# Ten weight slots in place of eight, GpSimd's transfers on SyncE's queue, and one weight split ahead of the memory scaling

## The reference

```python
xt = rms_norm(x, g_ffn)
logits = xt @ w_router + b_router            # 256 x 32
top_v, top_e = lax.top_k(logits, 4)
wts = softmax(top_v)
# for each expert e with its tokens:
hdn = xblk @ w_mlp1[e] + b_mlp1[e]           # 1024 -> 2048
x_glu = minimum(hdn[:, ::2], 7);  x_lin = clip(hdn[:, 1::2], -7, 7)
act = x_glu * sigmoid(1.702 * x_glu) * (x_lin + 1)
y += wts * (act @ w_mlp2[e] + b_mlp2[e])     # 1024 -> 1024
```

## Time and profile before

| what | value |
|---|---|
| median of 3 runs | 1199.2 us |
| the profiled execution | 1199.93 us |
| its span, first to last instruction | 1198.0 us (1.9 us lie around it) |
| TensorE matmul busy | 1151.2 us, 96% |
| VectorE, ScalarE, GpSimd busy | 403.2, 227.5, 36.9 us |
| moved by the 16 DMA engines | 454.87 MB |
| mean granted TensorE clock | 0.989 |

### The profile page before, as it was taken

The page is one execution under the profiler, slowest core; times in us unless marked ns, Lnnn a source line. Parts: engine busy times, 40 slices in busy tenths (PEclk is TensorE's granted clock), DMA queues, the critical chain, the costliest instruction groups (busy, mean ns, idle before and its releaser), DMA issues.

```text
span 1198.0 us, 13151 instructions
## 1 busy us (share of the span) xinstructions
PE 1151.2 (96%) x5373; PEld 540.1 (45%) x5373; DVE 403.2 (34%) x664; ACT 227.5 (19%) x353; POOL 36.9 (3%) x42
## 2 busy tenths in 40 slices
PE   9999999999999999999999999998999999999998
PEld 8788778874333333333333333333333333333332
DVE  4765666954222222232222223222222222222221
ACT  3445556531000000010110000000000000000001
POOL 0000332200000000000000000000000000000000
PEclk9999999999999999999999999999999999999999
DMA  9655655798999999999999999999999999999996
GB/s 346 227 182 182 194 177 171 252 412 363 405 432 429 420 422 433 426 434 426 432 431 427 435 425 433 427 431 432 427 433 425 432 429 430 426 428 428 427 428 271
DMA packets 46274, 454.87 MB, mean 380 GB/s; under 512 B 3696, under 2 KB 3856, under 8 KB 27088
## 3 DMA queue, kind: packets, MB, share of 16 engines
q1 hardware_dynamic: 44864, 450.21, 90.5%
q0 software_dynamic: 784, 2.38, 0.7%
q10 hardware_dynamic: 576, 1.51, 0.3%
HBM read 453.04 MB, written 1.05 MB: 379 GB/s over the span
## 4 chain that ended last, share of the span: by engine, by line
PE 65%; DMA 33%; DVE 1%; SPq 0%; issue 0%; ACT 0%; DVEq 0%
PE PS L1574 23%; DMA gate_raw<-in_w_mlp 18%; PE PS L1367 14%; PE PS L1582 11%; DMA raw<-in_w_mlp 10%; PE PS L1620 3%; PE PS L1549 3%; DMA head_raw<-in_w_mlp 2%; DMA gates<-in_memT 1%; PE PS L1398 1%; PE PS L1334 1%; PE PS L1556 1%; PE PS L1562 1%; PE PS L1607 1%; PE PS L1564 1%; PE PS L1383 1%
## 5 line engine op out<-in xcount | busy, mean ns | idle before, releaser
L1270 DVE TENSOR_SCALAR hT<-PS 128x512 f32<-128x512 f32 x32 | 22.1, 691 | 330.5 <-PE PS L1574 330.5
L1574 PE MATMUL PS<-value_raw,XG 128*64 128x512 f32 x544 | 123.8, 608 | 7.9 <-DMA value_raw<-in_w_mlp 7.9
L869 ACT ACTIVATE hT<-hT 128x512 f32<-128x512 f32 x31 | 19.5, 630 | 572.3 <-DVE hT L1270 572.3
L1574 PE MATMUL PS<-raw,XG 128*64 128x512 f32 x544 | 120.8, 595 | 6.7 <-DMA raw<-in_w_mlp 6.7
L1574 PE MATMUL PS<-head_raw,XG 128*64 128x512 f32 x480 | 111.4, 618 | 9.5 <-DMA head_raw<-in_w_mlp 9.4
L1574 PE MATMUL PS<-gate_raw,XG 128*64 128x512 f32 x480 | 108.3, 603 | 6.1 <-DMA gate_raw<-in_w_mlp 5.7
L951 DVE TENSOR_TENSOR rest<-raw,mix_hi 128x2048 fp32r<-128x2048 f32 x38 | 90.0, 2370 | 41.9 <-ACT mix_hi L718 41.8
L1212 DVE TENSOR_TENSOR X<-X,PS 128x512 f32<-128x512 f32 x120 | 74.6, 681 | 57.5 <-PE PS L1620 57.5
L1205 DVE COPY XG<-PS 128x512 f32<-128x512 f32 x32 | 22.1, 691 | 210.3 <-PE PS L1556 210.3
L718 ACT ACTIVATE mix_hi<-raw 128x2048 fp32r<-128x2048 f32 x38 | 72.7, 1914 | 39.3 <-PE PS L1367 29.6
L1574 PEld LDWEIGHTS PS<-value_raw,XG 128*64 128x64 f32 x544 | 38.7, 139 | 91.0 <-issue 79.7
(11 more groups left out here) (268 smaller groups left out, 1189.3 us busy)
## 6 DMA issues: line engine op xcount, KB each, us to landing
value_raw<-in_w_mlp SPq DMA_DIRECT2D x26, 2048.0 KB, 24.4
head_raw<-in_w_mlp SPq DMA_DIRECT2D x24, 2048.0 KB, 27.3
raw<-in_w_mlp SPq DMA_DIRECT2D x24, 2048.0 KB, 26.0
head_raw<-in_w_mlp SPq DMA_DIRECT2D x12, 4096.0 KB, 29.8
raw<-in_w_mlp SPq DMA_DIRECT2D x12, 4096.0 KB, 31.3
gate_raw<-in_w_mlp SPq DMA_DIRECT2D x22, 2048.0 KB, 30.4
gate_raw<-in_w_mlp SPq DMA_DIRECT2D x11, 4096.0 KB, 31.4
value_raw<-in_w_mlp SPq DMA_DIRECT2D x11, 4096.0 KB, 30.8
```

Of the source, the lines that this page charges most:

```text
L869: act.activation(sig, glu, ACT.Sigmoid, scale=ALPHA).then_inc(sgm, 1)
L1270: dve.tensor_scalar(glu, PS[:, 0:1024:2], LIMIT, None, ALU.min).then_inc(swi, 1)
L1574: mm = pe.matmul(PS[h * SL:(h + 1) * SL, n * 512:(n + 1) * 512], XG[:, 2 * u + c, :], tile[:, cols], start=False, stop=(u == W1U - 1 and c ...
```

## The change

The ring gets ten slots: a fifth tile, `low_raw`, holds slots 8 and 9. It overlaps the gate bias (now one tile, `gate_bias`), the router's tiles, `mT` and `gffn`. `EXTRA` is now slot 9 itself, loaded in two pieces; slot 8 is loaded in the mixer, behind unit 35; `HALVED` is now load 10, an "up" load. GpSimd issues no transfer any more: the gate bias comes as one transfer ahead of unit 8, the router's data ahead of unit 12, and the second bias behind `EXTRA`, all on SyncE's queue; `w_router` is laid out beforehand so that each partition's part is contiguous, and 1 KB is reserved for GpSimd's descriptors. VectorE scales the memory tokens behind the split of unit 5 instead of unit 4. At the end the two products for the first 128 tokens are each cut in two products of 64 rows, and those that don't need the last expert are done ahead of the wait.

```diff
-SLOTS_N = 8
+SLOTS_N = 10
-FIRST_ORDER = (3, 7, 0, 1, 2, 4, 5, 6)
+FIRST_ORDER = (3, 8, 7, 0, 1, 2, 4, 5, 6)
-HALVED = ("down", 0, 0)
+HALVED = LOADS[SLOTS_N]
...
+        low = ExitStack()
+        gate_bias = sb("gate_bias", [P, 3 * D], scope=low)
+        sb("low_rest", [P, D], scope=low)
+        wr = sb("wr", [P, KC, NE], scope=low)
+        sb("wr_rest", [P, 256], scope=low)
+        squares = sb("squares", [P, 512], scope=low)
...
+        mT = sb("mT", [P, KC, S], scope=low)
+        gffn = sb("gffn", [P, D], scope=low)
+        low.close()
+        low_tile = sb("low_raw", [P, 8192])
...
-        pairs = [gate_tile, value_tile, raw_tile, head_tile]
+        pairs = [gate_tile, value_tile, raw_tile, head_tile, low_tile]
...
+                elif slot == 8:
+                    sp.wait_ge(pair_sem("gate5"), GI["gate5"] // 2 + 1)
...
+                if m == UNITS_DONE[GI["br_moba0"]] + MIX_RING + 1:
+                    first_round(FIRST_ORDER[1])
                 if m == N_MIX - 1:
-                    first_round(FIRST_ORDER[1])
+                    first_round(FIRST_ORDER[2])
+                if m == UNITS_DONE[GI["cq"]]:
+                    sp.dma_start(gate_bias[:, :], a["b_gate"][0:1, :].to_broadcast([P, 3 * D])).then_inc(bias_in, 16)
+                if m == UNITS_DONE[GI["rv"]]:
+                    sp.dma_start(gffn[:, :], a["g_ffn"][0:1, :].to_broadcast([P, D])).then_inc(bcast_in, 16)
+                    sp.dma_start(brt[:, :], a["b_router"][0:1, :].to_broadcast([P, NE])).then_inc(bcast_in, 16)
+                    sp.dma_start(wr[:, :, :], a["w_router"].rearrange("p (k e) -> p k e", e=NE)).then_inc(bcast_in, 16)
+                    sp.dma_start(bsel[:, 0:NE], a["misc"][0:64, 4 * P + 64:4 * P + 64 + NE]).then_inc(bsel_in, 16)
...
+            late_home = ring[SLOT[EXTRA]].rearrange("p (k n) -> p k n", k=4)
             sp.wait_ge(lg_parts, 1)
-            sp.dma_start(mT_rows.rearrange("p (k n) -> p k n", k=2), rows[:, 1:3, :]).then_inc(extra_in, 16)
+            sp.wait_ge(sq_done, sum(SQUARES))
+            sp.dma_start(late_home[:, 0:3, :], rows[:, 0:3, :]).then_inc(extra_in, 16)
             sp.wait_ge(xt_done, 2 * TT)
-            sp.dma_start(extra[3], rows[:, 3, :]).then_inc(extra_in, 16)
-            sp.wait_ge(sq_done, sum(SQUARES))
-            sp.dma_start(extra[0], rows[:, 0, :]).then_inc(extra_in, 16)
+            sp.dma_start(late_home[:, 3, :], rows[:, 3, :]).then_inc(extra_in, 16)
+            sp.dma_start(b2s, a["b_mlp2"][0]).then_inc(b2_in, 16)
...
-                    if step[1] == SPLIT_UNITS[2]:
+                    if step[1] == SPLIT_UNITS[3]:
                         dve.wait_ge(memT_in, 16)
                         dve.wait_ge(hTl_done, 1)
                         dve.wait_ge(unit_used, 2)
...
+            def last_pair(item):
+                for n in range(2):
+                    half = (n + item) % 2
+                    rows = slice(half * SL, (half + 1) * SL)
+                    mm = pe.matmul(banks[LAST_BANK[0, n]], STL[rows, n * S:n * S + P], (Y, Y2)[n][rows, :],
+                                   start=(n == 1 and item == 0), stop=(item == 1))
+                    mm.then_inc(sc_pe if item else last_pair_done, 1)
...
             pe.wait_ge(st_act, j + 2)
+            pe.wait_ge(yc, j + 1)
+            last_pair(0)
             pe.wait_ge(yc, j + 2)
             pe.wait_ge(last_rows, 1)
-            for t, n in quarters:
+            pe.wait_ge(last_pair_done, 2)
+            last_pair(1)
+            for t, n in quarters[2:]:
...
-    nc = bacc.Bacc("TRN2", target_bir_lowering=False, num_devices=1)
+    nc = bacc.Bacc("TRN2", target_bir_lowering=False, num_devices=1, dynamic_dma_scratch_size=1024)
```

More of the change, by code:

```diff
@@ L95 @@
 assert not set(LAST_DOWN) & {SLOT[load] for load in LOADS[-IU:]}
-assert all(SLOT[load] % 2 == load[2] % 2 for load in LOADS) and LOADS[SLOTS_N + 1] == EXTRA
+assert all(SLOT[load] % 2 == load[2] % 2 for load in LOADS) and LOADS[SLOTS_N - 1] == EXTRA and HALVED[0] == "up"
 Q_GROUPS = ["rqk", "mq", "mk", "cq", "ck"]
@@ L233, in sb @@
             return scope.enter_context(nc.sbuf_tensor(name, shape, dt))
+        low = ExitStack()
[4 more added lines that the diff above has]
+        squares = sb("squares", [P, 512], scope=low)
+        first = ExitStack()
+        mTh = sb("mTh", [P, KC, S], F32R, scope=first)
+        first.close()
+        mT = sb("mT", [P, KC, S], scope=low)
+        gffn = sb("gffn", [P, D], scope=low)
+        low.close()
+        low_tile = sb("low_raw", [P, 8192])
         first = ExitStack()
@@ L289, in build @@
         BL = sb("BL", [P, 4, SL], F32R)
-        ends = sb("ends", [P, 128 + D + D + 384])
+        ends = sb("ends", [P, 1792])
         b2s = ends[0:NE, 128:128 + D]
@@ L300, in build @@
         hx = sb("hx", [P, TT, D])
[L301 to L304, removed]
         misc = sb("misc", [P, MISC])
@@ L406, in build @@
         part_high = sem("part_high")
-        bias_in = [sem(f"bias_in{i}") for i in range(2)]
+        bias_in, bsel_in = sem("bias_in"), sem("bsel_in")
         rout = sem("rout")
@@ L523, in first_round @@
                 kind, j, u = LOADS[slot]
-                load_w1_half(slice(j, j + 1), u, ring[slot], ring_in[slot])
+                (load_w1_half if kind == "up" else load_w2)(slice(j, j + 1), u, ring[slot], ring_in[slot])
             for m, (g, hk) in enumerate(UNITS):
@@ L580, in _ @@
                     tile, landed, _ = weight_tile(kind, j, u)
+                    rows = w1[j, 512 * (u // 2):512 * (u // 2) + 512, :].rearrange("(p k) n -> p k n", k=4)
                     sp.wait_ge(half_used, 1)
-                    load_w2_rows(slice(j, j + 1), u, tile, 0, 2, half_in)
+                    sp.dma_start(tile[:, 0:FF2], rows[:, 2 * (u % 2), :]).then_inc(half_in, 16)
                     slot_used(n - SLOTS_N)
-                    load_w2_rows(slice(j, j + 1), u, tile, 2, 2, landed)
+                    sp.dma_start(tile[:, FF2:2 * FF2], rows[:, 2 * (u % 2) + 1, :]).then_inc(landed, 16)
                     continue
@@ L646, in normalised @@
                 ins.then_inc(norm_done, 1)
[L648 to L654, removed]
-                if i >= 2:
-                    pool.wait_ge(pair_sem(f"gate{i - 2}"), GI[f"gate{i - 2}"] // 2 + 1)
-                if i == 6:
-                    continue
-                pool.dma_start(bg[:, i % 2, :], a["b_gate"][0:1, 512 * i:512 * i + 512].to_broadcast([P, 512])).then_inc(bias_in[i % 2], 16)
-            pool.wait_ge(pair_sem("gate5"), GI["gate5"] // 2 + 1)
-            pool.dma_start(b2s, a["b_mlp2"][0]).then_inc(b2_in, 16)
-            pool.dma_start(bsel[:, 0:NE], a["misc"][0:64, 4 * P + 64:4 * P + 64 + NE]).then_inc(b2_in, 16)
+            for h in range(NH):
+                normalised(h)
             pool.wait_ge(task_done, TASKS[("pv",) + out_block(NH - 1)] + 1)
@@ L1568, in up @@
                 tile, landed, count = weight_tile("up", j, u)
+                if isinstance(j, int) and ("up", j, u) == HALVED:
+                    pe.wait_ge(half_in, 16)
                 pe.wait_ge(landed, count)
@@ L1589, in down @@
                 if isinstance(j, int) and ("down", j, v) == EXTRA:
-                    rows, landed, count = extra, extra_in, 16 * 3
-                if isinstance(j, int) and ("down", j, v) == HALVED:
-                    pe.wait_ge(half_in, 16)
+                    landed, count = extra_in, 16 * 2
                 pe.wait_ge(landed, count)
```

26 lines of the change are left out of this document (9 added, 17 removed).

## The result

The changed kernel takes 1189.1 us (median of 4 runs, 1188.4 to 1189.6), the kernel before 1198.9 in the same session (4 runs, 1198.4 to 1199.5). The ratio is 0.9918 with a 95% interval of 0.99 to 0.9935: 9.8 us less, 1.1 us more than the 1188.0 forecast, and inside the range. The profiled execution took 1189.4 us with a span of 1187.5, 10.5 less than before's 1198.0; in what follows, spans are compared with spans.

What follows compares the result with a forecast made beforehand. The prediction took the DMA weight stream, not TensorE, to bound the kernel. Gains of 4.9 + 4.9 + 0.7 + 0.7 = 11.2 us took the median from 1199.2 to 1188.0 us, range 1184.5 to 1192.5.

Steps and rivals of the forecast that it cites:

- What bounds the kernel: Whole run: the DMA weight stream sets the end, at about 428 GB/s; TensorE has some 30 us of waits to give.
- Term 1: Late mixer, 218 to 236 us: slot 8's 2 MB load fits in free stream time, 4.9 us gained.
- Term 2: Early experts, holes at 286 to 292 and 300 to 304 us: mostly filled, 4.9 of 5.5 us gained.
- Term 3: Mixer, units 5 and 6: split ahead of scaling starts unit 6 2.3 us earlier, low clock takes 1.6; 0.7 us gained.
- The forecast's case: Mixer, unit 6: the lower clock behind its 2.0 us wait costs 1.6 us; forecast 1188.0 us, chance 0.56.
- the clock holds: Rival, mixer: unit 6 pays nothing for the lower clock, or the mixer gains all; 1186.4 us, chance 0.25.
- Term 4: Kernel's end: last products in row halves, 0.9 saved less 0.2 for overrun and semaphore; 0.7 us gained.
- The edits at nothing: Gate bias, router data, second bias moved to SyncE's queue, and GpSimd's normalisations: no cost, thanks to spare transfer time.
- Only one slot counts: Rival: the holes stay or slot 8 disturbs the last mixer units; 4.9 us less gain, 1192.9 us, chance 0.12.
- The slower stream: Rival, ten slots: up to ten outstanding loads lower the rate; 1.2% less eats everything, 1.5% gives 1202 us; chance 0.04.
- TensorE as the bound: Rival: TensorE sets the end, needing more than 29.7 us off the transfers; some 20 us of waits forecast left; chance 0.01.
- issue to landing of a pair of loads: Sign, late in the run: time from a load's issue to its landing longer by 10 us.

Runs made afterwards that it cites:

- the long hole: Changed kernel with the load behind `HALVED` waiting for unit 3 of expert 0 instead of unit 1: 1193.9 us, 0.9952.
- the short hole: Changed kernel with the load behind `HALVED` waiting for unit 2 of expert 0 instead of unit 1: 1190.3 us, 0.9926.
- e10: Kernel before (eight slots) with unit 5's split ahead of the memory scaling and ScalarE's unit 6 copy ahead of `mTh`: 1196.6 us, 0.9975.
- e7: Changed kernel, ten slots, with at most eight loads outstanding from load 60 on: 1188.8 us, 0.9915.
- e4: Changed kernel with ScalarE copying unit 6 ahead of making `mTh`, not behind it: 1186.3 us, 0.9895.
- the slot 8 kernel: Changed kernel with slot 8's load issued last in the first round, behind slot 6, not among the mixer's units: 1193.8 us, 0.9957.
- The base: The changed kernel itself, run again unaltered as the measure for variants: 1189.9 us, 0.9919.

## Why the prediction was right, step by step

**What bounds the kernel: right.** Room given back to the stream returned at the end at about its length: 4.0 to 4.6 us of 4.9 for slot 8, 4.8 of 5.9 for the long hole, and 2.9 for a start 3.2 us earlier. Only the short hole came out smaller in the time, 0.5 to 0.8 for 2.3. In the three profiles of the changed kernel the lead at 1160, counted from the experts' start, is 10.2, 10.3 and 10.5 us: what differs between them lies ahead of that start.

**Term 1, slot 8, 4.9: right.** The lead at 236 us is 4.9 us, the rate 300 GB/s for 295 forecast, and 4.0 to 4.6 us of time when it was undone. The price to unit 36 came out at the edge of what the prediction called covered: ScalarE now waited for the landing at 230.25, inside the 230 to 230.5 forecast, VectorE 0.68 us for ScalarE, and TensorE 0 to 0.3, once 1.55. Part of that is luck: the forecast had 5.8 to 6.3 us from unit 36's issue to its landing, and it was 7.2 to its copy (7.4 and 7.5 in the repeats), but the issue itself came 1.2 us earlier than before. The cover, "up to a microsecond", is real and nearly used up.

**Term 2, the holes, 4.9: right, if a little large.** The lead grows by 5.2 us between 236 and 320 us in the first profile; less the 1.1 by which the experts start earlier it is 4.1. Counted from the experts' start, the lead comes to 9.0 at 320 us for both terms, and 10.2 at 1160, where 9.8 was the sum. The 1.5 us from a load's issue to its start, an estimate, fits the trace of the kernel before: behind the load of 289.87 bytes move again from 290.8 us on, and at the full rate from 292.0, 0.9 and 2.1 us later. The reading that the load behind `HALVED` waits for unit 1 now is confirmed by the two kernels that made it wait for unit 2 and unit 3.

**Term 3, 0.7: right, by both its parts.** Over the eight profiled executions with this mixer and no other change to it, unit 6 starts at 45.7 to 47.0 us, at a mean of 46.3: 2.3 earlier than before, as worked out. In six of the eight the lower clock takes part of it back: from unit 6 to the experts they need 231.5 to 231.8 us, for 229.9 before and 230.1 and 230.2 in the two others. Some 1.7 us of 2.3 are lost, and 0.6 stay. The scatter is as large: in the first profile the experts start 1.1 earlier, in the two repeats 0.2 earlier and 0.35 later. The forecast's case and the rival "the clock holds" were both true, in different executions; the choice between them was one of frequency.

**Term 4, 0.7: mis-sized, 0.27.** Three steps failed, by 0.43 us together: the saving of the pair (0.9), the overrun and the semaphore (0.2), and the two whole products, which were taken as unchanged. One more row of the kernel before, TensorE's third of the four steps of the earlier trace rows, shows the sizes:

```profile
1192.54 1.02 PE L1705 MATMUL PS<-Y,ends 128*128 128x512 f32 x2
```

The products replaced took 1192.54 less 1190.74, 1.80 us, and the late pair takes 1.06: 0.74 gained for 0.9. The late pair begins 1.19 us behind the copy's start, where the products of before began after 0.83, so overrun and semaphore cost 0.36 and not 0.2. The two whole products left, with the addition's start behind them, take 2.02 us for 1.91, 0.11 more. That leaves 0.27. The kernel with the old products has 4.54 us there again, so the size is repeated, in profiles; the times are too coarse for it.

**What the sum lacked.** Two things that nearly cancel. Between 320 and 600 us the lead grows by another 0.9 (0.8 in both repeats), but not in the eight-slot kernel `e10` (2.6 at both), so it goes with the ten slots. In the kernel before, the stream still dipped to 380 GB/s at 390 to 400 us and to 400 at 420 to 430. Windows of 447 to 452 stand beside them, so over 380 to 450 us the mean is 424, for 428 in the changed kernel: (1 - 424/428) x 70 = 0.7 us. I had looked for holes near 300 us alone. And the lead at 1160 us is not all there at the last copy: 1.3 us go in the first profile, 0 to 1.5 in the others, 1.2 in `e7` and 1.1 in the eight-slot `e10`. So neither ten loads outstanding nor ten slots are needed for it, and it differs between executions of like kernels. It fits that before's one profile had an early last landing, but no run isolates that: what sets it stays open.

The measured parts of the first profile, 4.9 at 236 us, 5.2 by 320, 1.2 by 1160, less 1.3 at the end, and 0.5 for the tail and what lies behind it, are 10.5, as the span says; the median says 9.8.

**The edits at nothing: right, as far as the mixer shows.** No run takes the moved transfers alone, but `e10` has none of them, nor slot 8's load. It needs 230.1 us from unit 6 to the experts, and `e4`, the same order in the mixer with all of them, 230.2, both at full clock.

**Rivals.** "Only one slot counts" is what the slot 8 kernel shows, at 1193.8 for 1192.9 forecast, and the changed kernel isn't that. The slower stream is out (426 to 430 GB/s), TensorE as the bound too, though it kept 24.9 us of its waits and not the 20 forecast: it was busy 1147.0 us, for 1151.2. One of the signs named was off: issue to landing of a pair of loads grew by 2 to 6 us (page medians of 30 to 31 became 33 to 37), not 10.

## What to carry to other kernels

In a kernel that its weight stream bounds, count bytes: those moved ahead of the moment from which the stream is full, and the holes behind it. The sum of both, and of any earlier start of the whole, is the gain, and waits of TensorE in between don't enter. When a wait is removed, follow the chain on to the next operation that hangs on the same engines before booking it: here one more instruction put behind (ScalarE's `mTh`) was worth 2.9 us, where the edit that only moved the wait by a unit was worth 0.3 to 1.0. A load put ahead of others is free only up to their cover, and that cover has to be read at the landing, on more than one execution.

## What the runs showed of the hardware

The lower clock behind a short wait is not a matter of the wait's length alone in these runs. Behind waits of 1.98 to 2.47 us, units 6 and 7 took 12.6 to 12.8 us in six profiled executions and 11.1 to 11.2 in two, where the waits were 2.13 and 2.47; with 0.48 and 0.67 us it was 11.1 to 11.2. The expert phase of the kernel before says the same: in the 4 us behind its five waits of 2.34 or 2.35 us the granted clock was 0.57 to 0.60, and behind waits of 2.73 and 3.19 us (at 903.84 and 815.58) it was 1.00. What decides it, no run shows.

The base's two groups of times, 1.5 us apart, fit the two cases at unit 6. The mean granted clock that is on record for each execution fits too: of the fourteen of the changed kernel, the six with 0.994 took 1188.2 to 1188.8 us, the eight with 0.989 to 0.993 took 1189.1 to 1190.5. It is a mean over the whole span, slow stretches of the expert phase included, so it doesn't prove where the clock was low.

Ten outstanding loads of 2 MB moved bytes at the rate of eight: from 320 to 1160 us all fourteen profiles have 429 GB/s. The Trainium skill, "DMA: Bandwidth & Descriptors", section "Where 436 GB/s comes from", has some 358 GB/s as a core's limit. The same page gives that figure as each core's share when both cores of a memory domain stream; this kernel runs on one core, and none of the profiles is down at it.
